# Two kinds of matrix from one product: block transposes on VectorE in place of half of the TensorE products in a 64x64 triangular inversion

## What is computed

```
def step(S, inp):
    w_t, k_t, v_t, kk_t, a_t = inp[:5]
    sa = jnp.einsum('bhvk,bhk->bhv', S, kk_t)
    S = (S * w_t[:, :, None, :] - sa[..., None] * (kk_t * a_t)[:, :, None, :]
         + v_t[..., None] * k_t[:, :, None, :])
    y = jnp.einsum('bhvk,bhk->bhv', S, inp[5]) if emit else None
```

## Time and profile before

| | |
|---|---|
| median of 3 runs | 2807.09 us (2794.07 to 2812.53) |
| the profiled execution | 2801.8 us, its span 2799.8 us |
| PE busy | 2458.9 us, 88% of the span |
| DVE busy | 1430.8 us, 51% |
| ACT busy | 983.8 us, 35% |
| POOL busy | 612.7 us, 22% |
| granted TensorE clock, mean | 0.916 |
| `rwkv0_inv`, first ACT fill to last level-5 product | 527.05 to 592.47 us |
| `rwkv1_inv` | 694.52 to 763.83 us |
| `gdn0_inv` | 1203.03 to 1248.50 us |
| `gdn1_inv` | 1319.07 to 1363.66 us |

### The profile page before, as it was taken

One profiled execution on the slowest core, in us unless ns is written; L12 is line 12 of the kernel. 1 busy time (PEld: TensorE's weight loads), 2 busy tenths in 40 slices (PEclk: granted clock), 3 DMA queues, 4 the chain that ended last, 5 costly groups with the idle time before them and its releaser, 6 DMA issues. The chain is left out here.

```text
span 2799.8 us, 59935 instructions
## 1 busy us (share of the span) xinstructions
PE 2458.9 (88%) x25174; PEld 2041.2 (73%) x25174; DVE 1430.8 (51%) x2560; ACT 983.8 (35%) x1718; POOL 612.7 (22%) x335
## 2 busy tenths in 40 slices
PE   7967697786868899778878999999988898999998
PEld 3856585684855788668767888888876675688886
DVE  6788787537357855246543443144225464642341
ACT  3243224425343433543433232132224443332231
POOL 0000000100112222030213323222332201544444
PEclk9987798777589999999989999999999999999999
DMA  7521151000033633100031212111223202423232
GB/s 279 181 90 44 40 192 43 3 4 2 4 122 105 248 99 120 36 4 3 4 136 45 68 60 70 58 60 63 71 91 135 73 1 101 147 97 102 87 105 81
DMA packets 63138, 229.30 MB, mean 82 GB/s; under 512 B 6352, under 2 KB 12880, under 8 KB 60880
## 3 DMA queue, kind: packets, MB, share of 16 engines
q1 hardware_dynamic: 62928, 226.22, 23.4%
HBM read 211.52 MB, written 13.63 MB: 80 GB/s over the span
## 5 line engine op out<-in xcount | busy, mean ns | idle before, releaser
L2376 POOL TENSOR_TENSOR b_wl<-b_stage,b_wh 128x1024 fp32r<-128x1024 f32 (+1 forms) x72 | 186.6, 2591 | 476.6 <-ACT b_wh L2372 476.6
L2675 DVE SCALAR_TENSOR_TENSOR f_xr<-f_ps,cols,f_xr 128x511 f32<-128x511 f32 (+1 forms) x132 | 83.2, 658 | 327.7 <-ACT f_xr L2668 327.7
L2372 ACT ACTIVATE b_wh<-b_stage 128x1024 fp32r<-128x1024 f32 (+1 forms) x72 | 81.5, 1132 | 460.7 <-PE f_ps L2507 404.9
L2507 PE MATMUL f_ps<-h_h,b_wl 128*128 128x256 f32 (+1 forms) x672 | 226.3, 337 | 0.0
L2376 POOL TENSOR_TENSOR c_wl<-c_stage,c_wh 128x1024 fp32r<-128x1024 f32 (+1 forms) x68 | 178.4, 2624 | 218.1 <-ACT c_wh L2372 218.1
L2507 PE MATMUL f_ps<-h_h,b_wh 128*128 128x256 f32 (+1 forms) x672 | 226.1, 336 | 0.0
L2507 PE MATMUL f_ps<-h_l,b_wh 128*128 128x256 f32 (+1 forms) x672 | 225.8, 336 | 0.0
L2372 ACT ACTIVATE c_wh<-c_stage 128x1024 fp32r<-128x1024 f32 (+1 forms) x68 | 77.3, 1137 | 262.2 <-PE f_ps L2507 232.8
L2376 POOL TENSOR_TENSOR a_wl<-a_stage,a_wh 128x1024 fp32r<-128x1024 f32 x33 | 84.6, 2563 | 247.6 <-ACT a_wh L2372 247.6
L2507 PEld LDWEIGHTS f_ps<-h_h,b_wh 128*128 128x128 f32 x672 | 127.6, 190 | 13.6
L2507 PEld LDWEIGHTS f_ps<-h_l,b_wh 128*128 128x128 f32 x672 | 127.4, 190 | 13.5
(11 more groups left out here) (757 smaller groups left out, 6985.4 us busy)
## 6 DMA issues: line engine op xcount, KB each, us to landing
b_stage<-in_ffn_up SPq DMA_DIRECT2D x44, 512.0 KB, 3.2
c_stage<-in_ffn_up SPq DMA_DIRECT2D x44, 512.0 KB, 3.3
first_stage<-in_w_in SPq DMA_DIRECT2D x33, 512.0 KB, 3.7
a_stage<-in_ab_w SPq DMA_DIRECT2D x25, 512.0 KB, 3.6
p_hgrn_side_w<-in_ada_w SPq DMA_DIRECT2D x12, 1024.0 KB, 5.0
b_stage<-in_ffn_down SPq DMA_DIRECT2D x16, 704.0 KB, 4.1
c_stage<-in_ffn_down SPq DMA_DIRECT2D x16, 704.0 KB, 4.1
a_in_side_w<-in_ada_w SPq DMA_DIRECT2D x8, 1024.0 KB, 6.2
```

The lines of the kernel that those rows point to most:

```text
L2372: self.nc.scalar.activation(self.wh[:, slot, :w], self.stage[:, slot, :w], ACT.Copy).then_inc(self.w_high, 1)
L2376: self.nc.gpsimd.tensor_tensor(self.wl[:, slot, :w], self.stage[:, slot, :w], self.wh[:, slot, :w].bitcast(F32), ALU.subtract).then_inc(se ...
L2507: done = self.nc.tensor.matmul(out[s][:, :tn], w, x[:, k, t0:t0 + tn], start=k == 0 and n == 0, stop=k == job.kt - 1 and n == 2)
L2675: nc.vector.scalar_tensor_tensor(out, b[:, :n - 1], self.tap(part, 0, i), out, ALU.mult, ALU.add).then_inc(self.before_ok[part], 1)
```

## The change

For levels 1 to 4 the products of line 1410 are gone. TensorE makes only the new columns of the one form, and VectorE transposes it in blocks of 32x32 to get the other, which up to level 4 is the whole transpose. The starting transposes of line 1390 go the same way. `lower` becomes `low`, which has three slots of a part's half: the straight tiles, the across tiles as `upper` wants them (halves swapped back), and the across tiles as `product1` wants them. ACT writes the second slot first (`staged`) and then the third (`low_ok`); VectorE copies the first slot, waits for its own write (`low_x`) and for `staged`, and transposes both slots at once into `upper` (`turned`). The second product waits for `turned` of the level before.

```diff
@@ VectorE @@
-                nc.vector.copy_predicated(lower[:, second_half(u)], first, part[:, n:, :]).then_inc(placed, 1)
+                nc.vector.copy_predicated(low_of(u, 2, 3), first, part[:, n:, :]).then_inc(placed, 1)
+            for u in range(n_parts):
+                dve.wait_ge(placed, 2 * u + 2)
+                dve.wait_ge(crossed, 2 * u + 2)
+                nc.vector.transpose(low_of(u, 0, 2), upper[:, both(u)]).then_inc(turned, 1)
...
                     if lv < 5:
-                        nc.vector.tensor_copy(columns_of(lower[:, first_half(u)], lv, d), out_of(straight[u], u, 1, lv))
-                        nc.vector.tensor_copy(columns_of(upper[:, first_half(u)], lv, 1 - d), out_of(straight[u], u, 0, lv)
-                                              ).then_inc(straight_ok, 1)
+                        dve.wait_ge(product2, step + 1)
+                        nc.vector.tensor_copy(columns_of(low_of(u, 0, 1), lv, d), out_of(straight[u], u, 1, lv)).then_inc(low_x, 1)
+                        dve.wait_ge(low_x, step + 1)
+                        dve.wait_ge(staged, step + 1)
+                        nc.vector.transpose(upper[:, both(u)], low_of(u, 0, 2)).then_inc(turned, 1)
@@ ACT @@
+            for u in range(n_parts):
                 act.wait_ge(turned, u + 1)
                 act.wait_ge(crossed, 2 * u + 2)
-                for half, bank in ((first_half(u), straight[u]), (second_half(u), across[u])):
-                    ins = nc.scalar.activation(lower[:, half], bank[:, :C * n_of[u]].rearrange("p (a t) -> p a t", t=C), ACT.Copy)
-                ins.then_inc(crossed_ok, 1)
+                for c in range(2):
+                    ins = nc.scalar.activation(low_of(u, 2, 3)[rows64(c)], low_of(u, 1, 2)[rows64(1 - c)], ACT.Copy)
+                ins.then_inc(low_ok, 1)
...
                     if lv < 5:
-                        nc.scalar.activation(columns_of(lower[:, second_half(u)], lv, d), out_of(across[u], u, 1, lv), ACT.Copy)
-                        got = out_of(across[u], u, 0, lv)
+                        got = out_of(across[u], u, 1, lv)
                         for c in range(2):
-                            ins = nc.scalar.activation(columns_of(upper[rows64(c), second_half(u)], lv, 1 - d), got[rows64(1 - c)],
-                                                       ACT.Copy)
-                        ins.then_inc(crossed_ok, 1)
+                            ins = nc.scalar.activation(columns_of(low_of(u, 1, 2)[rows64(c)], lv, d), got[rows64(1 - c)], ACT.Copy)
+                        ins.then_inc(staged, 1)
+                        nc.scalar.activation(columns_of(low_of(u, 2, 3), lv, d), got, ACT.Copy).then_inc(low_ok, 1)
@@ TensorE @@
-            for u in range(n_parts):
-                pe.wait_ge(placed, 2 * u + 2)
-                for a, _, tile, bank, own, _ in each(u):
-                    src = upper if bank is straight[u] else lower
-                    done = nc.tensor.matmul(bank[own, a * C:(a + 1) * C], src[own, tile, :], ident[own, :], start=True, stop=True)
-                done.then_inc(turned, 1)
...
-                    pe.wait_ge(crossed_ok, at_step[u, lv] + 1)
+                    pe.wait_ge(low_ok, at_step[u, lv] + 1)
                     if lv > 1:
-                        pe.wait_ge(straight_ok, at_step[u, lv - 1] + 1)
+                        pe.wait_ge(low_x, at_step[u, lv - 1] + 1)
...
-                    if lv < 5:
-                        for a, _, tile, bank, own, far in each(u):
-                            nc.tensor.matmul(bank[own, (n + a) * 32:(n + a) * 32 + 32], upper[far, tile, :],
-                                             one(cx[far, lv % 2, tile, :], lv, d), start=True, stop=True)
+                    pe.wait_ge(turned, n_parts + at_step[u, lv - 1] + 1 if lv > 1 else u + 1)
                     for a, _, tile, bank, own, far in each(u):
-                        done = nc.tensor.matmul(bank[own, a * 32:a * 32 + 32], cx[far, lv % 2, tile, :],
-                                                one(upper[far, tile, :], lv, 1 - d), start=True, stop=True)
+                        if lv < 5:
+                            done = nc.tensor.matmul(bank[own, (n + a) * 32:(n + a) * 32 + 32], upper[far, tile, :],
+                                                    one(cx[far, lv % 2, tile, :], lv, d), start=True, stop=True)
+                        else:
+                            done = nc.tensor.matmul(bank[own, a * 32:a * 32 + 32], cx[far, lv % 2, tile, :],
+                                                    one(upper[far, tile, :], lv, 1 - d), start=True, stop=True)
```

More of the change, by code:

```diff
@@ L1251, in inverses64 @@
     with Stage(nc, name) as st:
-        lower = st.sbuf("lower", [P, n_tiles, C])
+        low = st.sbuf("low", [P, 3 * n_tiles // 2, C])
         upper = st.sbuf("upper", [P, n_tiles, C])
@@ L1255, in inverses64 @@
         filled, unit, placed, crossed, turned = (st.sem(s) for s in ("filled", "unit", "placed", "crossed", "turned"))
-        product1, picked, product2, straight_ok, crossed_ok = (
-            st.sem(s) for s in ("product1", "picked", "product2", "straight_ok", "crossed_ok"))
+        product1, picked, product2, low_ok, low_x, staged = (
+            st.sem(s) for s in ("product1", "picked", "product2", "low_ok", "low_x", "staged"))
         straight, across = st.banks("x", n_parts), st.banks("y", n_parts)
@@ L1273, in both, with low_of @@
             return slice(int(ends[u]) - 2 * n_of[u], int(ends[u]))
+        def low_of(u, first, last):
+            o = 3 * (int(ends[u]) - 2 * n_of[u]) // 2
+            return low[:, o + first * n_of[u]:o + last * n_of[u], :]
         def columns_of(ap, lv, child):
@@ L1335, in _ @@
             for u in range(n_parts):
-                for half, to in ((first_half(u), upper), (second_half(u), lower)):
-                    nc.scalar.activation(to[:, half], spread(ident, 1, n_of[u]), ACT.Copy).then_inc(filled, 1)
+                for to in (upper[:, first_half(u)], low_of(u, 2, 3)):
+                    nc.scalar.activation(to, spread(ident, 1, n_of[u]), ACT.Copy).then_inc(filled, 1)
             for u in range(n_parts):
@@ L1340, in _ @@
                 for c in range(2):
[L1341 removed]
+                    nc.scalar.activation(upper[rows64(c), second_half(u)], low_of(u, 2, 3)[rows64(1 - c)], ACT.Copy
                                          ).then_inc(crossed, 1)
+            for u in range(n_parts):
                 act.wait_ge(turned, u + 1)
                 act.wait_ge(crossed, 2 * u + 2)
[L1345 to L1347 removed]
+                for c in range(2):
+                    ins = nc.scalar.activation(low_of(u, 2, 3)[rows64(c)], low_of(u, 1, 2)[rows64(1 - c)], ACT.Copy)
+                ins.then_inc(low_ok, 1)
             for lv in range(1, 6):
@@ L1394, in _ @@
                     n = n_of[u]
-                    pe.wait_ge(crossed_ok, at_step[u, lv] + 1)
+                    pe.wait_ge(low_ok, at_step[u, lv] + 1)
                     if lv > 1:
-                        pe.wait_ge(straight_ok, at_step[u, lv - 1] + 1)
-                    for a, i, tile, bank, own, far in each(u):
-                        done = nc.tensor.matmul(bank[far, a * 32:a * 32 + 32], part[own, i, :], one(lower[own, tile, :], lv, d),
+                        pe.wait_ge(low_x, at_step[u, lv - 1] + 1)
+                    for a, i, _, bank, own, far in each(u):
+                        held = low_of(u, 2, 3) if bank is across[u] else low_of(u, 0, 1)
+                        done = nc.tensor.matmul(bank[far, a * 32:a * 32 + 32], part[own, i, :], one(held[own, a, :], lv, d),
                                                 start=True, stop=True)
```

6 lines of the change are left out of this document (2 added, 4 removed).

## The result

The changed kernel takes 2780.2 us (median of 6 runs, 2773.3 to 2785.5) against 2805.7 us (6 runs, 2794.1 to 2812.5). The ratio is 0.9909, 95% interval [0.9886, 0.9932]: 0.9% faster. The forecast was 2760 us, with 43.3 us of gain by its terms; 25.5 were found. The executions that were profiled took 2785.5 and 2801.8 us.

What follows compares the result with a forecast made beforehand. The prediction took TensorE's supply of instructions to bound these stages. Gains of 25.3, 7 and 11 us took the profiled 2801.8 us to 2758.5, put at 2760 us, with a range of 2736 to 2782.

Steps and rivals of the forecast that it cites:

- rival 1: VectorE sets the pace, a transpose costing twice the forecast price (1.25 and 1.9 us): 2778 us in all, chance 0.12.
- Term A: Levels 2 to 4 of both `rwkv` stages: 288 records a level instead of 432, 25.3 us gained.
- the seam's cover: Between two `rwkv` levels, TensorE's own products hide 0.3 us of VectorE's delay, otherwise paid once a level.
- Term B: Start and level 1 of `rwkv`: later `product1`, but 144 records instead of 288; 3.5 us gained a stage, 7 us together.
- Term C: `gdn` levels with 192 records instead of 288: 5.4 us gained a stage, 11 us together.
- Rivals 2 and 3: Transpose at upper price, no change, about 2804 us, chance 0.08; transpose far below copy rate, slower, 2845 us, chance 0.04.
- Rival 4: Every removed instruction block pays its time, also at the starts and in `gdn`: 70 us, 2734 us, chance 0.12.

Runs made afterwards that it cites:

- e4: The changed kernel with the removed products of levels 1 to 4 issued again on TensorE in all four inversions, results unused; 2822.8 us, ratio 1.0078.
- e6: As e4, but each of the added unused products has 1 moving column instead of 32; 2833.8 us, ratio 1.0106.
- e7: As e1, with VectorE transposing each part twice in levels 1 to 4, the first time into an unused tile; 2784.6 us, ratio 0.9941.
- e5: The changed kernel with a short start: VectorE turns each part straight after its masked copies, ACT's swaps come later; 2757.7 us, ratio 0.9831.
- e1: The changed kernel with TensorE's opener in the two `gdn` inversions lengthened from 2 to 8 products of 128x512; 2761.9 us, ratio 0.9854.
- e9: As e5, with an opener of 4 products instead of 2 in `gdn`; 2752.6 us, ratio 0.9828.
- e10: As e9, with one unused product of 128x512 added behind each of the first two groups of `product1` in `gdn`; 2752.6 us, ratio 0.9837.
- e2: As e1, and also an opener of 10 products instead of 2 in the two `rwkv` inversions; 2764.0 us, ratio 0.9856.

## Why the prediction was right in sign and too large

The time lies in the range, 1.8 us inside its upper end, and that is luck: the end had been set for transposes dearer than forecast (rival 1), and they were not. The prediction gave 0.83 to a time below 2779 us and 0.12 to one within 1% of no change, and 2780.2 us is of the second kind.

- **What bounds `rwkv`** held: instructions on TensorE. e4 and e6 give the time back with the same and with almost no columns, and the stops of over 0.8 us end behind the landing of an instruction packet.
- **Term A**, 25.3 us: 11.0 and 12.9 were measured, 23.9. A level of 288 records takes 8.7 and 8.9 us and not 8.02 and 9.12, so the price from level 5 (8.57 on average) was 0.2 us short. VectorE's 6.3 us a level measured 5.9 (17.8 / 3), the transpose 0.64 to 0.71 us against the 0.63 taken. The 0.1 us for the wait on its own write had no row in the prediction; in the changed kernel a transpose starts 0.29 us behind such a copy, where the second copy before started 0.21 us behind the first. e7 shows that the seam's cover is real: twice the transposes cost 1.6 us in three levels.
- **Term B**, 7 us: by the windows 2.2 and 2.5, 4.6 in sum. The chain of the start came as worked out: ACT's last swap ended 11.7 us after the stage's start (forecast 11.7), and the last products of level 1 ended at 17.0 (forecast 16.7). What I left out is that a level ends here with VectorE's copy of the last part, and VectorE, with its transposes queued up, came to it at 18.1 (549.61), 1.1 us behind the products. TensorE did not wait for that: its first product of level 2 came 3.1 and 3.4 us earlier in the stage than before, 6.5 in sum, and the rest is paid in level 2. e5 shows that more lay in the order of the start: 1.6 us ahead of the first masked copy and 1.2 in level 1.
- **Term C**, 11 us, is the step that failed: the stages lost 2.7 and 3.6 us. I priced level 2 at 17 ns a record, with the 1.00 of the earlier trace rows taken for granted, and levels 3 and 4 at level 5's 6.0 us. That price came from windows at 0.56 and 0.50, so for level 4, which has no `beside` product, it stood even at the low clock: 6.49 us. For level 3 I had put its two `beside` products at nothing. In `gdn0_inv` levels 1 and 2 together lost 3.5 us (0.3 gained in the forecast), level 3 lost 1.8 (2.9 gained), level 4 gained 1.7 (2.2), and level 5, which I had left as it was, 0.9. I had written that TensorE has nothing to do between its opening products and `product1` and "the clock ... may fall", and asked what that costs in `rwkv` alone, where it costs little. In `gdn`, whose levels carry `beside` products of 128x128, it costs 8.3 to 8.8 us a stage. With the clock kept, e1's stages are 6.1 and 4.7 us below those of before: 10.8 against the 11 of the forecast. That the two are so near is luck too, since they are differently spread: by the steps level 4 gave 2.9 and 3.4 us and level 5 1.4 and 0.3, the start took 1.1, and level 3 of `gdn0_inv`, cut as in the earlier trace rows, still took 7.64 us and not 6.0 with the clock at 1.00, so its `beside` products were not free there either:

```profile
1197.27:1204.91 7.64, 6.77 (x262) 4.78 (x260) 6.15 (x15) 5.04 (x17) 6.91 (x11) 1.00 0.02 4
```

- **The sum.** With the clock of C kept, e1 is 40.7 us below the kernel before, where 43.3 had been worked out. By stages it is 29.6 us in `rwkv` (32.3 forecast in A and B) and 10.8 in `gdn`.
- **Rival 1** (VectorE sets the pace) came near in its time, 2778, and not in its mechanism: transposes cost 0.71 us, not 1.25, and those of `gdn`'s levels, beside a busy GpSimd, took the same 0.71. Rivals 2 and 3 fall by the same row. Rival 4's idea that each removed block pays everywhere is met in levels 2 to 4 of `rwkv` alone.

What stays open: why the clock came back in one `gdn` stage of e4 and not in the other with the same code, why a wait of 2.0 us went with a fall in e9 and e10 and not in e1 and e2, and why `rwkv` levels at a clock of 0.50 vary from 8.3 to 9.3 us.

## What to carry to other kernels

Work taken off TensorE can be paid for with TensorE's clock: here 8.3 to 8.8 us a stage in `gdn`, more than the 6.1 and 4.7 us that the change won there with the clock kept. Where a change opens a gap, read the granted clock of the stage before and after, and ask what in it scales with the clock: the small products bound by instructions hardly did here (7.65 against 8.31 us a level), the large ones did (1.12 against 2.07 us). Fill the gap with products that nobody reads (e1), or reorder the preparation so that the first real product comes sooner (e5, which also gained 3.7 and 5.0 us in the `rwkv` stages; by the whole time e1 and e5 are not told apart). And a queue's work that is moved within a stage whose sum binds gains nothing by itself.

## What the runs showed of the hardware

- Products of 64x64 with 32 columns start 26 ns a record apart at 1.2 GHz (changed kernel, `rwkv1_inv`) and 14.7 ns at 2.4 GHz (its `rwkv0_inv`, and e2's level 1). With one column it is 25 ns at 1.2 GHz (e6): the number of columns hardly enters here.
- In long rows of such products 128 records take 3.8 to 4.0 us at 1.2 GHz (e4, and levels 2 to 4 of the changed kernel's `rwkv1_inv`) and 3.4 to 4.1 at 2.4 GHz (e2's level 1; the stops of the changed kernel), where stops of up to 1.9 us fill what the records save. The stops of 0.8 us and more end 1.3 to 1.6 us behind the landing of a 16 KB packet of instructions (changed kernel, `rwkv0_inv`).
- VectorE's transpose of 32-bit data takes 0.71 us for 128x512 and 0.98 us for 128x768, 0.64 and 0.91 us from start to start, and 0.71 also beside a busy GpSimd (level 2 of `gdn`); a masked copy of 256 columns takes 0.43 us alone and 0.84 beside GpSimd's fills (e5).
- TensorE's clock fell from 2.4 to 1.2 GHz in pauses of 4.77 us (changed kernel, e4), 7.2 us (`rwkv`) and 3.3 us (e7), each behind products of 128x512 or a level of small ones. Behind a pause of 2.0 us it fell in four stages (e9, e10) and stayed in four (e1, e2).
